# One loop for all experts, gate weights in whole rows, an early copy of the projections, and masked stores at the end, in a hybrid attention and mixture-of-experts step

## What is computed

```python
z = rms_norm(x) @ w_in          # pool branch | q1 q2 | k1 k2 | v | gate logits
attn = (softmax(q1 k1) - lam * softmax(q2 k2)) @ v      # 8 heads, rotary, chunk-causal mask
x = x + (sigmoid(gA) * (pool_y @ w_pool_branch) + sigmoid(gB) * (attn @ w_attn_branch)) @ w_out
t = rms_norm(x)                 # top-1 group of 4, then top-2 experts inside it
for e in range(16):
    hid = silu(t @ w_gate[e]) * (t @ w_up[e])           # 1024 -> 512
    y = y + combine[:, e:e + 1] * (hid @ w_down[e])     # 512 -> 1024
x = rms_norm(x + y)
```

## Time and profile before

| | us |
|---|---|
| median of three runs | 888.29 |
| lowest, highest | 887.80, 889.53 |
| the profiled execution's own time | 890.09 |
| its span, first to last instruction | 888.3 |
| PE busy in it | 834.4 |
| DVE busy, ACT busy | 603.9, 518.5 |

### The profile page before, as it was taken

The page is one execution under the profiler, slowest core; times in us unless marked ns, Lnnn a source line. Parts: engine busy times, 40 slices in busy tenths (PEclk is TensorE's granted clock), DMA queues, the critical chain, the costliest instruction groups (busy, mean ns, idle before and its releaser), DMA issues.

```text
span 888.3 us, 15492 instructions
## 1 busy us (share of the span) xinstructions
PE 834.4 (94%) x4963; PEld 737.7 (83%) x4963; DVE 603.9 (68%) x1026; ACT 518.5 (58%) x965; POOL 83.7 (9%) x73
## 2 busy tenths in 40 slices
PE   4999999999999999999999998999999999999891
PEld 3999999899989898989997887878777787778670
DVE  6363233687778778466555137689999898998684
ACT  7243214566656666455623232488888788878584
POOL 0000000000000000000000001122233222321020
PEclk9999999999999999999999999999999999999896
DMA  8622222133123212331236746599999999999974
GB/s 260 153 75 80 75 69 72 57 103 85 45 73 102 84 49 78 120 95 49 96 95 210 230 175 228 175 308 337 323 344 342 344 340 338 339 333 335 339 258 156
DMA packets 154392, 163.77 MB, mean 184 GB/s; under 512 B 20596, under 2 KB 138484, under 8 KB 154346
## 3 DMA queue, kind: packets, MB, share of 16 engines
q1 hardware_dynamic: 148538, 151.12, 52.1%
q0 software_dynamic: 5520, 11.45, 4.7%
q10 hardware_dynamic: 288, 0.59, 0.2%
HBM read 151.61 MB, written 20.12 MB: 193 GB/s over the span
## 4 chain that ended last, share of the span: by engine, by line
PE 48%; DVE 5%; DMA 2%; SPq 2%; issue 2%; ACT 1%; POOLq 0%; POOL 0%; DVEq 0%; ACTq 0%
PE ps L1542 14%; PE ps L1544 13%; PE ps L1543 13%; SPq L493 2%; DMA rawM<-in_w_expert_up 1%; PE ps L1906 1%; PE ps L1828 1%; PE ps L1926 1%; PE ps L1835 1%; DVE ob L1513 1%; DMA xg<-h_rows,idi 0%; PE ps L1820 0%; PE ps L1859 0%; DVE wl L1458 0%; PE ps L1860 0%
## 5 line engine op out<-in xcount | busy, mean ns | idle before, releaser
L1458 DVE TENSOR_TENSOR wl<-rawM,wh 128x1024 fp32r<-128x1024 f32 x189 | 223.6, 1220 | 25.3 <-ACT wh L913 23.5
L913 ACT ACTIVATE wh<-rawM 128x1024 fp32r<-128x1024 f32 x192 | 196.0, 1054 | 10.8 <-PE ps L1544 9.0
L1542 PE MATMUL ps<-hTh,wh 128*128 128x272 f32 x448 | 132.2, 295 | 1.6 <-ACT qkv L773 0.9
L1544 PE MATMUL ps<-hTh,wl 128*128 128x272 f32 x448 | 130.4, 291 | 0.0
L1543 PE MATMUL ps<-hTl,wh 128*128 128x272 f32 x448 | 129.7, 289 | 0.0
L1542 PE MATMUL ps<-wh,xh 128*128 128x512 f32 x256 | 105.3, 412 | 4.3 <-issue 4.3
L1543 PE MATMUL ps<-wl,xh 128*128 128x512 f32 x256 | 102.2, 399 | 0.0
L1544 PE MATMUL ps<-wh,xl 128*128 128x512 f32 x256 | 102.2, 399 | 0.0
L1542 PE MATMUL ps<-wh,hTh 128*128 128x384 f32 x256 | 94.5, 369 | 5.1 <-ACT qkv L773 3.6
L1542 PEld LDWEIGHTS ps<-hTh,wh 128*128 128x128 f32 x448 | 85.3, 190 | 3.3 <-ACT qkv L773 1.3
L1544 PE MATMUL ps<-wh,hTl 128*128 128x384 f32 x256 | 86.5, 338 | 0.0
(11 more groups left out here) (300 smaller groups left out, 1682.0 us busy)
## 6 DMA issues: line engine op xcount, KB each, us to landing
rawM<-in_w_expert_gate SPq DMA_DIRECT2D x128, 256.0 KB, 5.2
rawM<-in_w_expert_up SPq DMA_DIRECT2D x128, 256.0 KB, 7.4
rawM<-in_w_expert_down SPq DMA_DIRECT2D x64, 512.0 KB, 8.2
rawA<-in_w_in SPq DMA_DIRECT2D x64, 192.0 KB, 3.0
rawA<-in_w_in SPq DMA_DIRECT2D x20, 512.0 KB, 5.5
rawA<-in_w_attn_branch SPq DMA_DIRECT2D x8, 512.0 KB, 4.1
rawA<-in_w_out SPq DMA_DIRECT2D x8, 512.0 KB, 4.2
x<-in_x_prompt SPq DMA_DIRECT2D x4, 512.0 KB, 6.8
```

What stands on the lines that cost most here:

```text
L913: nc.scalar.activation(wh[:, (c + 1) % S, :], rawM[:, slot, :], ACT.Copy).then_inc(m_hi, 1)
L1458: V.tensor_tensor(wl[:, sl, :], rawM[:, slot, :], wh[:, sl, :].bitcast(F32), ALU.subtract).then_inc(m_lo, 1)
L1542: T.matmul(out, sh, mh_, start=start, stop=False, **kw)
L1544: return T.matmul(out, sl, mh_, start=False, stop=stop, **kw)
```

## The change

- `evacuate` takes a range of tiles. For each head, the copy of tile 0 moves ahead of the last step's turned probabilities and exponentials on ACT.
- Chunks 0 to 3 of an expert now hold the gate weights in whole rows (2 row blocks by 512 columns, one transfer); chunks 4 and 5 hold the first 256 up columns, 6 and 7 the second 256 (4 row blocks by 256 columns, one transfer). Gate goes to bank 0 with 512-column products; up goes to banks 1 and 7 with 256-column products.
- Silu runs once per item, over 512 columns. DVE multiplies each half ahead of the low part of the next chunk; the low parts of chunks 7 to 12 are interleaved anew.
- PE's items 0 and 1 become part of the loop, which now starts at 0; `xg_lo` counts in twos for this.
- At the end four roots and three scaled tiles stand ahead of the last expert's rows (three and two before). SP stores only the first three tiles. POOL stores the last expert's rows once those three have landed, and then tiles 2 and 3 with an index per row that is out of bounds where the row belongs to the last expert. Three small DVE instructions in the routing make these indices.

```diff
-                if c < 8:
-                    half, q = divmod(c, 4)
-                    d = d.rearrange("p (k m n) -> p k m n", k=2, m=2)
-                    for m in range(2):
-                        src = moe_src[m][e, 2 * P * q:2 * P * (q + 1), 256 * half:256 * (half + 1)]
-                        sp.dma_start(d[:, :, m, :], src.rearrange("(k p) n -> p k n", p=P)).then_inc(m_raw[slot], 16)
+                if c < 4:
+                    sp.dma_start(d.rearrange("p (k n) -> p k n", k=2), moe_src[0][e, 2 * P * c:2 * P * (c + 1), :].rearrange(
+                        "(k p) n -> p k n", p=P)).then_inc(m_raw[slot], 16)
+                elif c < 8:
+                    half, q = divmod(c - 4, 2)
+                    sp.dma_start(d.rearrange("p (k n) -> p k n", k=4),
+                                 moe_src[1][e, 4 * P * q:4 * P * (q + 1), 256 * half:256 * (half + 1)].rearrange(
+                                     "(k p) n -> p k n", p=P)).then_inc(m_raw[slot], 16)
                 else:
...
-            for j, t in enumerate(FINAL):
+            for j, t in enumerate(FINAL[:3]):
-            sp.wait_ge(f_out, 16 * NT)
+            sp.wait_ge(f_out, 16 * 3)
+            sp.wait_ge(f_late, 16 * 2)
...
-            pool.wait_ge(f_out, 16 * NT)
+            pool.wait_ge(f_out, 16 * 3)
             pool.wait_ge(y15_done, 2)
...
+            for j in (3, 4):
+                t = FINAL[j]
+                pool.wait_ge(f_done, j + 1)
+                pool.indirect_dma_start(o["y_prompt"][0], bass.IndirectOffsetOnAxis(ap=kept[:, ORDER.index(t):ORDER.index(t) + 1], axis=0),
+                                        ob[:, t, :], None, bounds_check=SEQ - 1, oob_is_err=False).then_inc(f_late, 16)
...
-            def evacuate(h):
-
-                for t in range(NT):
+            def evacuate(h, tiles=range(NT)):
+
...
                 if split_next is not None:
                     split_next()
+                if early is not None:
+                    early()
                 if 1 <= s <= NT:
                     kb = s if s < NT else 2
...
-                    step(g, s, (lambda: nxt(5)) if s == 2 else None)
+                    step(g, s, (lambda: nxt(5)) if s == 2 else None, early if s == NT - 1 else None)
...
-                attend(h - 1, lambda k: hi_head(k % 4, n + k, h + k // 4, WH if k == 3 else w_next))
-                evacuate(h)
+                attend(h - 1, lambda k: hi_head(k % 4, n + k, h + k // 4, WH if k == 3 else w_next),
+                       early=lambda: evacuate(h, (0,)))
+                evacuate(h, range(1, NT))
...
+                act.wait_ge(m_mm, n0 + 5)
+                act.wait_ge(hid_done, 2 * i + 1)
+                nc.scalar.activation(hsl[:], ps[:, 0, :], ACT.Silu).then_inc(si_done, 1)
                 for half in range(2):
-                    act.wait_ge(m_mm, n0 + 4 * half + 5)
-                    act.wait_ge(hid_done, 2 * i + half + 1)
-                    nc.scalar.activation(hsl[:, 256 * half:256 * half + 256], ps[:, half, 0:256], ACT.Silu).then_inc(si_done, 1)
-                    for c in ((7, 8) if half == 0 else (10,)):
+                    for c in ((7, 8, 9) if half == 0 else (10, 11)):
                         ahead(c)
                     act.wait_ge(hid_mm, 2 * i + half + 1)
                     nc.scalar.activation(hh[:, 2 * half:2 * half + 2, :],
                                          ps[:, 4, 256 * half:256 * half + 256].rearrange("p (k n) -> p k n", k=2),
                                          ACT.Copy).then_inc(hid_hi, 1)
-                    for c in ((9,) if half == 0 else (11, 12)):
-                        ahead(c)
+                ahead(12)
...
+            place = ps[:, 7, 0:NT * EXPERTS].rearrange("p (t e) -> p t e", t=NT)[:, :, EXPERTS - 1]
+            link(V.scalar_tensor_tensor(out=keep[:], in0=place, scalar=float(P), in1=ra[1][:, :, EXPERTS - 1],
+                                        op0=ALU.is_lt, op1=ALU.mult))
+            link(V.scalar_tensor_tensor(out=keep[:], in0=keep[:], scalar=float(4 * NO_ROW),
+                                        in1=cst[:, C_LIST:C_LIST + NT], op0=ALU.mult, op1=ALU.add))
+            V.tensor_scalar(kept[:], keep[:], float(NO_ROW), None, ALU.add)
...
-                for half in range(2):
+                def hidden(half):
+                    hs = slice(256 * half, 256 * half + 256)
+                    if half == 0:
+                        dve.wait_ge(si_done, i + 1)
+                    dve.wait_ge(m_mm, n0 + 2 * half + 7)
+                    V.tensor_tensor(hid[:, hs], ps[:, UP_BANKS[half], 0:256], hsl[:, hs], ALU.mult).then_inc(hid_done, 1)
+
+                def hidden_lo(half):
                     hs = slice(256 * half, 256 * half + 256)
                     kk = slice(2 * half, 2 * half + 2)
-                    dve.wait_ge(si_done, 2 * i + half + 1)
-                    V.tensor_tensor(hid[:, hs], ps[:, half, 256:512], hsl[:, hs], ALU.mult).then_inc(hid_done, 1)
-                    for c in ((7, 8) if half == 0 else (10,)):
-                        ahead(c)
                     dve.wait_ge(hid_hi, 2 * i + half + 1)
                     V.tensor_tensor(hl[:, kk, :], ps[:, 4, hs].rearrange("p (k n) -> p k n", k=2),
                                     hh[:, kk, :].bitcast(F32), ALU.subtract).then_inc(hid_lo, 1)
-                    for c in ((9,) if half == 0 else (11, 12)):
-                        ahead(c)
+                ahead(7)
+                hidden(0)
+                ahead(8)
+                hidden_lo(0)
+                ahead(9)
+                hidden(1)
+                ahead(10)
+                hidden_lo(1)
+                ahead(11)
+                ahead(12)
...
-                        k = 2 * (c % 4) + kk
-                        wc = slice(512 * kk, 512 * kk + 512)
-                        ins = three(ps[:, c // 4, :], xh[:, k, :], xl[:, k, :], wh[:, (c + 1) % S, wc], wl[:, (c + 1) % S, wc],
-                                    k == 0, k == KD - 1)
+                    rows, width = (2, 512) if c < 4 else (4, 256)
+                    bank = 0 if c < 4 else UP_BANKS[(c - 4) // 2]
+                    for kk in range(rows):
+                        k = rows * (c % 4 if c < 4 else c % 2) + kk
+                        wc = slice(width * kk, width * kk + width)
+                        ins = three(ps[:, bank, 0:width], xh[:, k, :], xl[:, k, :], wh[:, (c + 1) % S, wc],
+                                    wl[:, (c + 1) % S, wc], k == 0, k == KD - 1)
                     ins.then_inc(m_mm, 1)
...
-                for c in range(6):
-                    if first and c == 0:
-                        pe.wait_ge(xg_lo, 1)
-                    elif c == (2 if first else 0):
-                        pe.wait_ge(xg_lo, i + 2)
+                for c in range(7):
+                    if c == 0:
+                        pe.wait_ge(xg_lo, 2 * i + 1)
+                    elif c == 2:
+                        pe.wait_ge(xg_lo, 2 * i + 2)
                     up(c)
                 turn_hidden(0)
-                up(6)
                 up(7)
...
-            item(0, 0, first=True)
-            item(0, 1)
-            with pe.Fori(1, EXPERTS // 2 - 1) as ip:
+            with pe.Fori(0, EXPERTS // 2 - 1) as ip:
```

More of the change, by code:

```diff
@@ L66 @@
 NO_ROW = 1024
+UP_BANKS = (1, 7)
 UW = BUF + SEQ + BUF + DEC
@@ L165, in build @@
         over = small("over", [P, 1], I32)
+        keep = small("keep", [P, NT])
+        kept = small("kept", [P, NT], I32)
         ids = small("ids", [P, 1], I32)
@@ L760, in hi_head @@
                 nc.scalar.activation(wh[:, sl, 0:w], rawA[:, sl, 0:w], ACT.Copy).then_inc(hi_done, 1)
-            def evacuate(h):
-                for t in range(NT):
+            def evacuate(h, tiles=range(NT)):
+                for t in tiles:
                     if t < 4:
@@ L779, in square, with step @@
                                      accum_out=ssb[:, t, bass.ds(g, 1)]).then_inc(sq_done, 1)
-            def step(g, s, split_next=None):
+            def step(g, s, split_next=None, early=None):
                 if s < NT and not (isinstance(g, int) and g == 0):
@@ L810, in step, with attend @@
                     ins.then_inc(exp_done, 1)
-            def attend(g, nxt, gate_blocks={}):
+            def attend(g, nxt, gate_blocks={}, early=None):
                 act.wait_ge(acc_ev, NT * (g + 1))
@@ L1013, in _ @@
             act.wait_ge(m_lo, 24 * ip + 19)
-            for j in range(3):
+            for j in range(4):
                 final_root(j)
@@ L1515, in _ @@
             dve.wait_ge(gb_in, 48)
-            for j in range(2):
+            for j in range(3):
                 final_rows(j)
@@ L1531, in _ @@
             V.tensor_scalar(yb[:, 0, 512:D], xg[:, 1, 512:D], root15[:], None, ALU.mult).then_inc(y15_done, 1)
-            for j in range(2, NT):
+            for j in range(3, NT):
                 final_rows(j)
@@ L1903, in gathered @@
                     return
```

(4 more changed lines are left out.)

14 lines of the change are left out of this document (6 added, 8 removed).

## The result

Median of four runs of the changed kernel: 878.64 us (877.68 to 880.41), beside 888.91 (887.80 to 889.62) for the kernel before; ratio 0.9892, 95% interval 0.9876 to 0.9907. Forecast were 885.3 and a range of 878.5 to 889.8: the direction came out, the size was more than three times the forecast's 3.0 us. That the time lies inside the range, by 0.1 us, is luck: the low end stood there for a stop that shrinks or goes, which gave a small part of the gain. The profiled execution took 878.95 us with a span of 876.5. Two executions of one kernel can differ by some us (by 5.7 at most here), so in the experiments ratios and traces are read beside the medians.

What follows compares the result with a forecast made beforehand. PE was taken to bound the kernel, busy 256 of 256 us while experts run. Terms -3.5 + 1.5 - 1.0 = -3.0 us, taken off the median 888.29, gave 885.3 us; range 878.5 to 889.8.

Steps and rivals of the forecast that it cites:

- The early copy: Head boundaries: copying tile 0 early saves PE 0.52 us each, tile 1's wait subtracted; -3.5 us in all.
- The products of an expert: PE in the items: two up products of 256 columns cost 3.5 ns more than one of 512; +1.5 us.
- The line through 512 and 272 columns: PE product spacing: a line through these two measured widths gives 0.1182 us for a product of 256 columns.
- The bound from below: PE products: if 256 columns sit on a 0.109 us floor, a pair costs 0.218 and the change is -5.8 us.
- Handovers inside an item: Items, ACT and DVE to PE: no new wait, little room; 0, bounds 0 to +4 us.
- The tight way: From a turn over two DVE steps back to PE: 1.3 to 1.4 us within one 1.5 us chunk; no wait.
- The stop: PE's gap at item 14 and the slow clock behind it: both left as they are; 0, bounds -7.2 to +7.
- The loads: Expert weight transfers: faster by nothing to a few per cent; gain 0, as the wait ends inside item 14's stop.
- The end: Final tiles and POOL's stores: last store starts 2.4 us earlier but carries a whole tile; -1.0 us, bounds -2.5 to +0.5.
- Routing: Three small DVE instructions, about 0.7 us together, fall where DVE is idle for 3.35 us; 0.
- xg_lo in twos: Gathered rows: same values waited for, in the same order; 0.
- The rival of a shrinking stop: Item 14: code behind the jump is already there, up to 7.2 us more gained, 878.1 us; chance 0.2.

Runs made afterwards that it cites:

- experiment 1: Changed kernel with the early copy undone, all five copies of a head's projections behind the exponentials again: 882.04 us, ratio 0.9925.
- experiment 5: Changed kernel with the Silu cut in two halves again, the second only when chunk 7 is done: 882.53 us, ratio 0.9929.
- experiment 4: Changed kernel with ACT's high part of chunk 11 moved back behind the copy of the second turned half: 883.62 us, ratio 0.9934.
- experiment 2: Kernel before with DVE's low part of chunk 7 moved ahead of the first half of hid: 898.59 us, ratio 1.0109.
- experiment 3: Kernel before with ACT's high part of chunk 11 moved ahead of the copy of the second turned half: 890.24 us, ratio 1.0006.
- experiment 12: Kernel before with lighter loads, a sixth of the bytes of experts 2 to 15 left out: 887.74 us, ratio 0.9973.
- experiment 14: Kernel before with the changed kernel's end and its three routing instructions alone: 888.41 us, ratio 0.9990.
- experiment 11: Changed kernel with lighter loads, a sixth of the bytes of experts 2 to 15 left out: 879.14 us, ratio 0.9893.
- experiment 15: Changed kernel with PE's items 0 and 1 written out ahead of the loop again: 877.73 us, ratio 0.9868.

## Why the prediction was right and wrong

- *The early copy*: right in mechanism, place and sign. What I subtracted for tile 1 is there: its first product now starts 0.39 us behind the one before it instead of 0.17, and from the last product of a head to the first product of the attention behind the boundary PE takes 1.54 us instead of 2.08, 0.53 less, against 0.52 forecast. From head to head it is 0.57; where the other 0.04 comes from isn't traced. 4.0 in the traces, 3.4 in experiment 1, against 3.5.
- *The products of an expert* failed in size and sign, and were the largest single miss. The line through 512 and 272 columns gave 0.1182 for 256, and that is one of the two spacings found; but in the loop's items three of four up chunks ran at 0.1133, so a pair costs 0.2267, less than 0.2333. In twelve items each of 18 pairs saves 6.7 ns and each of 6 costs 2 to 3 ns; in the other four items all 24 cost 2 to 3 ns: about -1.1 us where I had +1.5, a miss of 2.6. So the line between two neighbours didn't carry to 256 columns for most of them. The bound from below (0.109) had held it. The Trainium skill, TensorE: Matmul & The Clock Gate, section Back-to-back issue gap, gives 262 cycles for 256 columns, 0.109 us at 2.4 GHz; no two of the experts' products of 256 columns started that close here, 0.113 at the least.
- *Handovers inside an item* is the step whose mechanism failed. I asked only whether a handover would get tighter, put the term at 0 and set the bounds 0 to +4, because PE showed 256 busy us of 256. The handover to the next item was already late in the kernel before, by 0.11 us each time, 1.5 us over 14 handovers, and 0.5 more were lost in the last item; together -2.0 where I had 0. The early Silu with the new order on ACT cured it. In the changed kernel, taking back the early Silu costs 1.8 us in the trace and 3.9 in the medians, taking back ACT's order 4.4 and 5.0 (experiments 5 and 4). I excluded a gain without a reason. The tight way that I did look at, a turn over L975 and L1470 back to PE, cost nothing, as forecast.
- *The stop* stayed, as forecast, over the same jump of 5.83 us. It still shrank: PE's sequencer reached the jump at 814.5 with 2.6 us of products still to issue, instead of 823.0 with 1.7. The low part that PE needs ahead of the jump ends earlier against need (the two DVE rows under the result). Gap -0.8, half clock -1.6 at most; the item with the stop fell by 1.8 in all, from 25.31 to 23.50. In the other traces it takes 24.25 to 25.26 us (experiments 2, 3, 12 and 14, variants of the kernel before) and 23.01 to 23.98 (1, 11 and 15, of the changed kernel with its own orders and no slower loads): 1.4 between the means. The half clock behind the stop is spread of single executions: it lasts 6.8 us in one trace and 3.4 in another with the same PE instructions.
- *The loads* were put at 0, from "faster by nothing to a few per cent", and it was 3%. In the kernel before they cost 1.9 us (experiment 12), though every wait in its trace lay under the stop; in the changed one nothing; and at the changed kernel's pace the old form costs 5.8, for the gate weights alone. The cover of one execution isn't the cover of all, and the price of a supply that is just enough grows with the speed of its user.
- *The end*: -1.0 forecast; measured alone -0.9 in the medians, -1.3 in the trace. Of its parts these hold: the rows start 1.1 us later against PE's last product, POOL starts on ACT's release and not on a landing, stores 1.3 to 1.7 apart.
- *Routing*, *xg_lo in twos*: nothing to see, as forecast. The rest of the traces' difference ahead of the experts, 1.0 us, goes with the clock: half clock for 6.8 us at the routing before, 3.4 after. No edit explains it, and variants of either kernel show both.

The terms as measured (copy 3.4 to 4.0, handovers 2.0, products 1.1, stop about 1.4, end 0.9 to 1.3, loads up to 1.9) add up to 9 to 12, and the medians to 10.3; how much of the loads' 1.9 is in it stays open. The rival of a shrinking stop was the nearest in its time, and wrong in its cause: the code behind the jump still wasn't there.

## What to carry to other kernels

Where an engine shows no idle time, compare the spacing of starts across each handover with the normal one before you call it bound by its own work: 0.11 us repeated 14 times stood in no list of waits. When supply and demand are within a few per cent of each other, price the supply against the new pace, not the old one. And before taking out a stop on the critical engine, look for what else ends at that time: of 5.2 us, 1.4 came through, and with lighter loads 3.7, since the weight transfers held the scatter and the load or gather behind it.

## What the runs showed of the hardware

- Products of 256 columns follow each other at either 0.1133 or 0.1178 us for a whole stretch of an item; what decides it is open. Products of 512 took 0.233 in both cases.
- DMA rows of 2 KB instead of 1 KB in a third of the weights moved 344 GB/s instead of 333 with the engines busy all the time (12 transfers per expert against 16; with 20 and rows of 1 KB it was 334).
- A taken jump over the unused body held PE's sequencer 5.83 us before and after, 4.47 to 6.61 in the variants and 4.85 to 6.61 with identical PE instructions; a loop whose end is a register, left by not jumping back, held it not at all.
